# Second feed-forward of a two-block transformer kernel by one level of Strassen, activations and residual through DRAM

## The reference, cut to what matters

```python
def mlp(s, shift, scale_m):
    hm = rms_norm_2(s, g_norm2) * (1.0 + scale_m) + shift      # (1024, 1024)
    return jnp.square(jax.nn.relu(hm @ w_mlp1)) @ w_mlp2        # (1024, 4096), then (1024, 1024)
x_new = x_new + gt2 * mlp(x_new, sh2, sc2)                      # the output
```

## Time and profile before

| what | value |
|---|---|
| three runs | 3763.41, 3763.51, 3774.17 us; median 3763.51 |
| profiled execution, span of the core | 3778.2 us (its own run time is not listed apart; the slowest run shown is 4.0 us under this span) |
| PE busy | 3606.1 us, 95% of the span |
| DVE, ACT, POOL busy | 1848.7, 1185.7, 702.7 us |
| mean granted TensorE clock | 0.972 of 2.4 GHz |
| second feed-forward | from 3049.4 us to the end |

### The profile page before, as it was taken

The page is one execution under the profiler, slowest core; times in us unless marked ns, Lnnn a source line. Parts: engine busy times, 40 slices in busy tenths (PEclk is TensorE's granted clock), DMA queues, the critical chain, the costliest instruction groups (busy, mean ns, idle before and its releaser), DMA issues. The chain is left out here.

```text
span 3778.2 us, 46616 instructions
## 1 busy us (share of the span) xinstructions
PE 3606.1 (95%) x18410; PEld 2808.8 (74%) x18410; DVE 1848.7 (49%) x3350; ACT 1185.7 (31%) x2093; POOL 702.7 (19%) x532
## 2 busy tenths in 40 slices
PE   7999999999999999999988988988999999999998
PEld 6756778888888888876557878646788468888886
DVE  4276992223685554244468884469321142232322
ACT  3155771222311211132434553128311032211210
POOL 1162000010101111010020110119201213333333
PEclk9999999999999999998998996999999999999999
DMA  3100111112233222113011212200122111111111
GB/s 131 38 2 25 42 39 56 53 56 78 89 95 109 92 90 95 51 60 123 1 22 33 46 34 72 78 17 2 26 73 64 56 54 47 45 56 45 45 56 45
DMA packets 266342, 211.67 MB, mean 56 GB/s; under 512 B 65680, under 2 KB 231184, under 8 KB 265744
## 3 DMA queue, kind: packets, MB, share of 16 engines
q1 hardware_dynamic: 264368, 201.61, 17.3%
q10 hardware_dynamic: 1760, 7.08, 0.9%
HBM read 185.33 MB, written 21.50 MB: 55 GB/s over the span
## 5 line engine op out<-in xcount | busy, mean ns | idle before, releaser
L95 PE MATMUL ps<-halves 128*128 128x512 f32 x10408 | 2408.2, 392 | 18.8 <-DVE halves L1542 6.6
L95 PEld LDWEIGHTS ps<-halves 128*128 128x128 f32 x10408 | 1957.1, 188 | 441.4 <-issue 26.9
L95 PE MATMUL ps<-arena 128*128 128x512 f32 (+2 forms) x1040 | 397.1, 540 | 11.6 <-issue 6.0
L95 PEld LDWEIGHTS ps<-arena 128*128 128x128 f32 x1040 | 199.4, 213 | 172.4 <-issue 160.3
L1521 POOL TENSOR_TENSOR tmps<-tmps 128x512 f32<-128x512 f32 x128 | 143.5, 1121 | 981.4 <-ACT tmps L1489 981.4
L1542 DVE TENSOR_TENSOR halves<-tmps,halves 128x512 fp32r<-128x512 f32 x128 | 89.0, 698 | 433.4 <-ACT halves L1497 433.4
L1425 ACT ACTIVATE halves<-raws 128x2048 fp32r<-128x2048 f32 x62 | 118.4, 1910 | 554.7 <-PE ps L95 532.5
L1528 POOL TENSOR_TENSOR arena<-arena 128x512 f32<-128x512 f32 x128 | 164.7, 1294 | 191.4 <-DVE arena L1569 191.4
L1489 ACT ACTIVATE tmps<-ps 128x512 f32<-128x512 f32 x128 | 76.6, 598 | 364.0 <-PE ps L95 354.0
L1569 DVE TENSOR_TENSOR arena<-ps,arena 128x512 f32<-128x512 f32 x128 | 87.7, 690 | 194.6 <-PE ps L95 188.5
L1365 DVE SCALAR_TENSOR_TENSOR arena<-arena,sc 128x128 f32<-128x128 f32 x448 | 163.4, 365 | 15.9
(11 more groups left out here) (300 smaller groups left out, 3548.7 us busy)
## 6 DMA issues: line engine op xcount, KB each, us to landing
raws<-in_w_ff SPq DMA_DIRECT2D x31, 1024.0 KB, 6.5
raws<-in_w_mlp SPq DMA_DIRECT2D x31, 1024.0 KB, 5.3
mixw<-in_w_in SPq DMA_DIRECT2D x56, 512.0 KB, 4.0
arena<-in_w_ada SPq DMA_DIRECT2D x48, 512.0 KB, 3.9
arena<-in_w_in SPq DMA_DIRECT2D x5, 2048.0 KB, 8.8
arena<-in_x SPq DMA_DIRECT2D x8, 1024.0 KB, 8.2
h_stash<-arena SPq DMA_DIRECT2D x1, 5120.0 KB, 20.6
inverses<-arena ACTq DMA_DIRECT2D x20, 256.0 KB, 2.9
```

Of the source, the lines that this page charges most:

```text
L95: ins = e.matmul(out_ap, l, r, start=i == 0, stop=i == n - 1)
```

## The change

It replaces the second block's `*_ff` by `*_up` and `*_down`.

**Up.** Jobs 0, 1, 14 and 15 stay as 16 plain units. Jobs 2 to 13 ("quads") each multiply the 256 columns with all tokens by Strassen's scheme in Winograd's form: 7 products of 12 matmuls in place of 8. The token side needs T1 to T4, made once from "joined" (high plus low) quarter blocks of 128x2048; the weight side needs S1 to S4 per job, four 128x512 operations on POOL, which then have to be split too (128x1536 on ACT and on DVE). The products go to four banks; DVE reads them in five 128x512 steps of PSUM with SBUF, ACT clips and POOL squares. Where a bank holds a sum of two products, the second (P2, P4, P3) waits until DVE has read the first. Every activation tile (128x512) is stored to DRAM by SP, and so is X at the start (`xm`), whose place in SBUF is used for weights.

**Down.** The 4096 rows are cut in four pieces cc of 1024. For each, 7 slots of 4 banks x 12 matmuls (28 slots g in place of 16 jobs of 96 matmuls). Both sides, activations (A) and weights (B), are loaded as 128x2048 blocks. B blocks are multiplied by the gate on DVE (four 128x2048 a piece), POOL makes the 8 sums (128x2048 each), ACT makes the high and DVE the low halves (two 128x2048 a slot on each). DVE adds each PSUM tile into X or into U2; at the end POOL adds U2 into X in 12 operations of 128x512. The output goes out in 16 stores of 256 KB as its tiles are done.

```diff
+        SEVEN = (1,)
+        QUADS = range(2, 14)
...
+            for h in range(2):
+                e.wait_ge(*x_added(blk, 4 * h + 3))
+                e.dma_start(xm[:, 4096 * h:4096 * h + 4096], R(F0 + 4096 * h, 4096)).then_inc(*l_xs[h].tick())
+            for h in range(2):
+                e.wait_ge(*l_xs[h].at(2 * nth7(blk) + 1))
+            e.wait_ge(*n_xn.at(NORMS[INST[blk]][5] + 8))
+            sync_up_load(e, blk, 2)
...
+                else:
+                    e.wait_ge(*up_end(blk, i - 1))
+                    sync_up_load(e, blk, i + 1)
+                if i > 2:
+                    sync_quad_store(e, blk, i - 1, "C12")
+                for c in ("C22", "C11", "C21"):
...
+            if opens:
+                e.wait_ge(*bk.vacant(key))
+            elif p == "P2":
+                e.wait_ge(*bk.clear(("qb", blk, i)))
+            elif p == "P4":
+                e.wait_ge(*u_v.at(blk, i, "U3"))
+            else:
+                e.wait_ge(*u_v.at(blk, i, "C22"))
...
+                if x == 2:
+                    tensor_norm(e, INST[blk], 4, FFX[INST[blk]], on_v)
+                if x == 4 and blk == 1:
+                    tensor_row(e, 1, TM2)
+                tensor_unit(e, blk, x)
+            for i in QUADS:
+                for p in ("P1", "P6", "P7", "P5", "P2", "P4", "P3"):
+                    tensor_product(e, blk, i, p)
+            for x in range(8, 16):
+                tensor_unit(e, blk, x)
...
+            vector_up_weights(e, blk, 1)
+            vector_norm_split(e, INST[blk], 4, gcol, scol)
+            if blk == 1:
+                vector_row(e, 40, TM2)
+            vector_tokens_join(e, blk)
+            vector_tokens_sum(e, blk, "T1")
+            vector_up_weights(e, blk, 2)
+            vector_tokens_sum(e, blk, "T3")
+            vector_tokens_sum(e, blk, "T2")
+            vector_up_sums(e, blk, 2)
...
+            for i in QUADS:
+                if i > 2:
+                    vector_quad(e, blk, i - 1, "C12")
+                for c in ("U2", "U3", "C22"):
+                    vector_quad(e, blk, i, c)
+                vector_up_weights(e, blk, i + 1)
+                if i + 1 in QUADS:
+                    vector_up_sums(e, blk, i + 1)
+                vector_quad(e, blk, i, "C21")
...
+            for x in range(8):
+                gpsimd_unit(e, blk, x)
+                if x in (0, 1):
+                    gpsimd_tokens_join(e, blk, ("11", "21")[x])
+                elif x == 3:
+                    gpsimd_weight_sums(e, blk, 2)
+                elif x in (4, 5):
+                    gpsimd_tokens_join(e, blk, ("T3", "T4")[x - 4])
+            for i in QUADS:
+                if i > 2:
+                    gpsimd_square(e, blk, i - 1, "C12")
+                if i + 1 in QUADS:
+                    gpsimd_weight_sums(e, blk, i + 1)
+                for c in ("C22", "C11", "C21"):
+                    gpsimd_square(e, blk, i, c)
+            gpsimd_square(e, blk, 13, "C12")
+            for x in range(8, 16):
+                gpsimd_unit(e, blk, x)
+                if x in (8, 9, 10, 11):
+                    gpsimd_down_sum(e, blk, 0, ("S1", "S2", "S3", "T1")[x - 8])
...
+        SLOTS7 = [("d1", "11", "11"), ("d1", "12", "21"), ("d6", "S2", "T2"), ("d7", "21", "12"), ("d7", "22", "T4"),
+                  ("d5", "S1", "T1"), ("d5", "S4", "22")]
...
+            e.wait_ge(*up_end(blk, 15))
+            for side, n in (("A", "12"), ("B", "21"), ("B", "22")):
+                sync_down_load(e, blk, side, 0, n)
+            sync_unit_store(e, blk, 15)
+            e.dma_start(R(F0 + 4096, 4096), xm[:, 4096:8192]).then_inc(*l_xs[1].tick())
...
+            for g in range(28):
+                cc, s = divmod(g, 7)
+                name, l, r = SLOTS7[s]
+                for side in "AB":
+                    e.wait_ge(*v_lo.at(blk, g, side))
...
+            if g >= 2:
+                e.wait_ge(*slot_end(blk, *divmod(g - 2, 7)))
...
+            e.wait_ge(*v_hi.at(blk, g, side))
+            if g == 1:
+                e.wait_ge(*up_end(blk, 15))
+            elif (side, n) in READERS:
+                e.wait_ge(*v_s.at(blk, cc, READERS[side, n]))
+            e.tensor_tensor(down_lo_block(Q3, side, g), down_raw(side, cc, n),
+                            down_hi_block(plain3, side, g), ALU.subtract).then_inc(*v_lo.mark(blk, g, side))
...
+        SCALE_AT = {1: "12", 2: "11", 3: "22", 5: "21"}
+        def vector_down(e, blk):
+            for n in ("12", "11"):
+                vector_down_scale(e, blk, 0, n)
+            for side in "AB":
+                vector_down_lo(e, blk, 0, side)
+            for g in range(28):
+                cc, s = divmod(g, 7)
+                if g == 0:
+                    vector_down_scale(e, blk, 0, "22")
+                    vector_down_scale(e, blk, 0, "21")
+                vector_down_lo(e, blk, g + 1, "A")
+                vector_down_tile(e, blk, cc, s, 0)
+                vector_down_lo(e, blk, g + 1, "B")
+                for q in range(1, 4):
+                    vector_down_tile(e, blk, cc, s, q)
...
+        SUMS7 = {"S1": ("A", "21", "22", ALU.add), "S2": ("A", "S1", "11", ALU.subtract),
+                 "S3": ("A", "11", "21", ALU.subtract), "S4": ("A", "12", "S2", ALU.subtract),
+                 "T1": ("B", "12", "11", ALU.subtract), "T2": ("B", "22", "T1", ALU.subtract),
+                 "T3": ("B", "22", "12", ALU.subtract), "T4": ("B", "21", "T2", ALU.subtract)}
+        SUM_PLACE_FREE = {"S1": 2, "T1": 2, "S2": 3, "T2": 3, "S4": 5, "T4": 5}
...
+            if cc and n in SUM_PLACE_FREE:
+                e.wait_ge(*slot_end(blk, cc - 1, SUM_PLACE_FREE[n]))
...
+        READERS = {("A", "11"): "S3", ("A", "12"): "S4", ("A", "22"): "S1", ("A", "S1"): "S2", ("A", "S2"): "S4",
+                   ("B", "11"): "T1", ("B", "21"): "T4", ("B", "22"): "T3", ("B", "T1"): "T2", ("B", "T2"): "T4"}
...
+        FIRST7, LATER7 = ("S1", "S2", "S3", "T1", "T2", "S4", "T4", "T3"), ("S1", "T1", "S2", "T2", "S3", "T3", "S4", "T4")
...
+            for n in FIRST7[4:]:
+                gpsimd_down_sum(e, blk, 0, n)
+            for cc in range(1, 4):
+                for n in LATER7:
+                    gpsimd_down_sum(e, blk, cc, n)
+            for i, k in PIECE_ORDER[1:]:
+                gpsimd_down_merge(e, blk, i, k)
...
+            if cc == 3 and s >= 4:
+                e.wait_ge(*v_m.at(blk, i, k, q))
...
-            sync_ff(e, 1)
-            e.wait_ge(*f_ad.at(128))
-            e.dma_start(x_of(out), X).then_inc(*l_out.tick())
-            e.wait_ge(*l_out.at(1))
+            sync_up(e, 1)
+            sync_down(e, 1)
+            for i, k in PIECE_ORDER:
+                for q in range(4):
+                    t = 4 * (2 - i) + q
+                    e.wait_ge(*down_done(1, i, k, q))
+                    e.dma_start(out[t * 128:t * 128 + 128, (k - 1) * 512:k * 512], down_x(i, k, q)).then_inc(*l_out.tick())
+            e.wait_ge(*l_out.at(16))
```

More of the change, by code:

```diff
@@ L88, in emptying, with __init__, tick, at @@
         return emptied.tick()
-def chain(e, out_ap, pairs):
+class Again:
+    def __init__(self, count, ended):
+        self.count, self.ended, self.sem, self.step, self.n = count, ended, count.sem, count.step, 0
+    def tick(self):
+        self.n += 1
+        return self.sem, self.step
+    def at(self, k):
+        return self.count.at(self.ended + k)
+class Marks:
+    def __init__(self, count, keys):
+        self.count = count
+        self.nth = {key: i + 1 for i, key in enumerate(keys)}
+    def at(self, *key):
+        return self.count.at(self.nth[key])
+    def mark(self, *key):
+        assert self.count.n + 1 == self.nth[key], (key, self.count.n, self.nth[key])
+        return self.count.tick()
+def chain(e, out_ap, pairs, first=True):
     n = len(pairs)
     for i, (l, r) in enumerate(pairs):
-        ins = e.matmul(out_ap, l, r, start=i == 0, stop=i == n - 1)
+        ins = e.matmul(out_ap, l, r, start=first and i == 0, stop=i == n - 1, skip_group_check=not first)
     return ins
@@ new lines, in build @@
+        first7 = R(21504, 512)
+        C_AT = {"C11": (0, 0), "C12": (0, 1), "C21": (1, 0), "C22": (1, 1)}
+        l_st = {c: Again(x, 2) for c, x in zip(ST, l_x)}
+        by_quad = lambda *names: [(b, j, n) for b in SEVEN for i in range(2, 15) for n in names
+                                  for j in ([i - 1] if n == "C12" else [i]) if j in QUADS]
+        u_v = Marks(Again(r_sq, 16), [(b, i, n) for b in SEVEN for i in QUADS for n in ("U3", "C22")])
+        u_r = Marks(Again(r_y, 8), by_quad("C12", "P1", "C22", "C21"))
@@ new lines, in build @@
+        u_sq = Marks(Again(r_rc, 8), by_quad("C12", "C22", "C11", "C21"))
+        q_ea, q_ev = a_ea, a_ev
+        UP_UNITS = [(i, m, 0) for i in (0, 1) for m in range(2)] + [(i, m, 1) for i in (0, 1) for m in range(2)] + \
+            [(i, m, h) for i in (14, 15) for h in range(2) for m in range(2)]
+        NTH = {u: x for x, u in enumerate(UP_UNITS)}
```

(64 more changed lines are left out.)

470 lines of the change are left out of this document (462 added, 8 removed).

## The result

**Result.** The kernel before took 3768.7 us (median of 9 runs, 3761.2 to 3774.2) and the changed kernel 3787.3 us (median of 9, 3776.1 to 3797.3). The ratio is 1.0048, 95% interval 1.0033 to 1.0064: slower by half a per cent, 18.6 us by the medians.

The account below looks back on a forecast made before the run. PE's count of matmuls was taken to set the time. Matmuls saved in the quads (-32.6), start (+12.2), down (+32.9) and ends (-5.1, -9.8) gave -2.4 us: 3761.1 us, called no change, range 3695 to 3797.

Parts of the forecast that it names:

- PE's own work: Whole feed-forward: 336 matmuls fewer, 76.1 us, of which 32.6 in the quads and 43.5 in down.
- The start: Start of the stage to job 2: POOL's joins and weight sums delay the gate's row and P6; +12.2 us, bounds 0 and 20.
- Up, steady: Quad jobs: the other engines' work and the loads fit within PE's 19.03 us a job; costed at nothing.
- second rival: Quad jobs: C12's store lands later than 10 us into a job, making P2 late; 42 us, 3803 us; 0.17 shared with the third.
- DVE and POOL exclude each other: Mostly down: operations with both inputs in SBUF wait for the other engine's whole instruction; POOL's sum 4.5 us, DVE's 2.15.
- Down, steady: Down's later pieces: PE stops ahead of slots 4, 5, 6 and 0; 94.4 us a piece against 76.2.
- The first piece: Down's first piece: DVE waits for B22's late load; slot 1 starts 30.1 us after slot 0 in place of 10.9.
- Ends: Ahead of the last down jobs a stop goes, -5.1 us; after the last tile a smaller store, -9.8 us.
- Sum: Whole kernel: -32.6 + 12.2 + 32.9 - 5.1 - 9.8 = -2.4 us, giving 3761.1 us, no change.
- first rival: Mainly down: POOL's long operation doesn't hold DVE out, or the order falls kinder; 3686 us, half way 3724; chance 0.28.
- third: Down's stopped slots: the clock loss after each stop isn't absorbed; 3780 us; 0.17 shared with the second rival.
- the pair's chain: Down's pieces, likeliest case, 0.55: DVE's and POOL's SBUF operations alternate without a break, 8 x 4.5 + 11 x 2.2, 60.0 us.

## Why the prediction was wrong

The feed-forward stage of the two profiled executions took 728.8 us before and 743.3 after, 14.5 us more; the forecast was 2.4 less, so 16.9 us are to be explained. Step by step:

- **PE's own work**: right, 336 matmuls fewer. Where PE doesn't stop, the last 336 take 76.4 us, 0.2275 us each against 0.2266.
- **The start**: right. The gate's row came 4.8 us later in the stage (forecast 4.7), and P6 waited 4.77 us (forecast 5). The clock loss behind it was larger: the 288 matmuls after it took 68.0 us against 65.3 at full clock, 2.7 us in place of 1.8.
- **Up, steady**: *the step that failed*. "I cost steady up at nothing; the cover is this slack." Before, down's matmuls began 366.5 us into the stage (728.8 less the 14.2 behind PE's end and 348.1 of down). With -32.6, +12.2 and -5.1 the first slot of down was to start at 341.0; it started at 360.5, 19.5 us late. That is made of nine stops (13.9 us, the row of L1959 above), 0.3 us after each of the eight short ones, 2.3 after the long one, and the 0.9 that the start lost more. With the one store moved behind the load the same slot starts at 343.3. The step put the load's issue "at the end of the job before last". In SP's list it stands behind C21's store, and C21's tile stands on DVE behind the low halves of the load before. I had added up each engine's work in a job (7.5 us of DVE, 10 of POOL) and found slack; I hadn't followed the list round to see whether it closes. The loads of the quads also take 6.7 to 6.8 us (medians), not 5.3, with stores of 256 KB about them in the queue. Those 1.5 us are as large as the whole excess of a job, 1.4; whether the loop would have fitted with loads of 5.3, no run shows.
- The **second rival** named the symptom, P2 late because C12's store lands late, with its place and its threshold: 10 us into a job. It lands about 11 us in. Its price, 42 us, was twice too high: in a closed loop a job loses only the loop's excess of 1.4 us, a stop of 1.1 and 0.3 behind it (at a granted clock of 1.00), where the rival reckoned 2 and 1.8. Its cause was also wrong in part, as two places for C12 show: without that wait the pitch stays at 20.4 us.
- **DVE and POOL exclude each other** and **Down, steady**: right. Slots within 0.1 us of the forecast, periods of 94.1 and 94.4 us against 94.4. The last period was 92.8, with only 0.3 us lost behind its last stop. The runs bear out the cause: without the sums no stop, cut in four 91.9, out of DVE's way 79.7. Down took 379.6 us against 381.0.
- **The first piece**: right, 18.5 against 19.2. The loads land and the gates run as stepped through.
- **Ends**: right, 3.2 us from the last tile against 4.4. By medians alone it couldn't have been shown.
- **Sum**: -2.4 + 19.5 - 1.4 - 1.2 = 14.5 us, as in the two traces. So the other terms held each by itself, and the miss is not a balance of errors. The medians' 18.6 has the scatter of runs of some 20 us in it.
- The **first rival** (the pair binds less) is excluded by the low halves' mean of 3.6 us, and the **third** (clock stays down) by the granted clock: after the 5.33 us stop it is 0.50 for the first 6 us of the slot and 1.00 in the rest and in the next slot, of 11.16 us. The sign that I gave for it, slots of over 12.7 us, was badly chosen: slots 4 took 13.0 to 14.0, so a stop of 5 us costs 2.2 to 3.1, not 1.8, and the pair's chain absorbed it all the same.

## What to carry to other kernels

Adding up each engine's work per iteration doesn't show that an iteration fits: follow each in-order list from a load to the next load of the same kind, and where the path closes, add up its latencies. When DVE and POOL both work on SBUF operands, what counts is which operation meets which, so a wait that keeps POOL's long operation out of DVE's urgent ones can save more than moving or cutting work. When the profile names the wait that PE stands at, take it away alone before believing that it is the bound.

## What was not expected of the hardware

- A DVE operation that comes while POOL's sum is running waits for its end and then takes its own time: the sum of 3479.30 ends at 3483.94, and the DVE sum issued at 3480.94 ends at 3486.09, 2.15 us later. A fill of the same 128x2048 tile on POOL (1.81 us) costs DVE little or nothing: the low halves beside such fills have a median of 2.29 us.
- Cutting the 128x2048 sum in four raises what it takes on POOL from 6.3 to about 8.1 us (the two groups of POOL's parts in that run, 148.1 + 47.3 us for 24 sums). Each part can be made to wait anew; that this is the reason is inferred, not shown.
- A stop of about 1 us costs some 0.3 us afterwards (84 matmuls in 19.33 us, against 19.03), and not by the clock: the granted clock is 1.00 in such rows. One of 4.96 costs 2.3 (276 in 64.79 against 62.54), with a granted clock of 0.69 in the first 6.65 us. In the quads the short stops cost no clock; the time of the stop itself is nearly all that they cost.
